# An eleventh expert buffer in a routed-expert decoder kernel, made from a smaller descriptor ring of the software queue

## The reference, cut to what matters

```python
h = h + mix                                  # retention, then dilated attention
hn = rmsnorm(h, ffn_norm[layer])
# per expert e, for the tokens routed to it:
hid = jax.nn.silu(xk @ w_gate[e]) * (xk @ w_up[e])     # 1024 -> 512
y   = hid @ w_down[e]                                  # 512 -> 1024
h = h + (sum of a token's two experts, weighted by the gates)
```

## Time and profile before

| | |
|---|---|
| median of 3 runs | 1400.17 us (1399.46 to 1400.95) |
| the profiled execution, first to last instruction | 1398.8 us |
| PE busy | 1075.8 us (77%) |
| DVE, ACT, POOL busy | 439.9, 343.5, 65.2 us |
| bytes moved, mean rate | 489.02 MB, 350 GB/s |
| mean granted TensorE clock | 0.899 of full |
| chain that ended last: DMA, PE | 46%, 45% of the span |

### The profile page before, as it was taken

How to read it: one execution, slowest core, us unless ns; L and a number is a source line. 1 busy time by engine, 2 the same in 40 slices (tenths; PEclk the granted TensorE clock), 3 DMA queues, 4 the chain that set the end, 5 groups by cost and what they waited for, 6 DMA issues and landing times.

```text
span 1398.8 us, 15978 instructions
## 1 busy us (share of the span) xinstructions
PE 1075.8 (77%) x6816; PEld 624.8 (45%) x6816; DVE 439.9 (31%) x863; ACT 343.5 (25%) x563; POOL 65.2 (5%) x120
## 2 busy tenths in 40 slices
PE   8999999666547666587999999999666646666586
PEld 8887885222212122132788877775222212122131
DVE  6845526010100101002876666736010100101001
ACT  4334524100001000011655555534100001000010
POOL 2000000000000000000300016300000000000000
PEclk9999999878888788899999999999988879788889
DMA  9655589999999999999755547699999999999997
GB/s 340 237 180 181 221 339 348 427 427 427 429 427 428 427 427 428 427 424 399 220 186 180 180 153 165 169 378 414 430 427 427 428 428 427 427 429 427 428 422 295
DMA packets 75785, 489.02 MB, mean 350 GB/s; under 512 B 6112, under 2 KB 6320, under 8 KB 51136
## 3 DMA queue, kind: packets, MB, share of 16 engines
q1 hardware_dynamic: 71296, 480.53, 84.6%
q0 software_dynamic: 4000, 7.36, 2.8%
q10 hardware_dynamic: 416, 0.07, 0.0%
HBM read 486.77 MB, written 1.17 MB: 349 GB/s over the span
## 4 chain that ended last, share of the span: by engine, by line
DMA 46%; PE 45%; DVE 3%; ACT 2%; issue 1%; SPq 1%; POOL 0%; DVEq 0%; ACTq 0%
DMA ring<-in_exp_up 11%; PE quad L1414 9%; DMA ring<-in_exp_gate 9%; PE quad L380 8%; PE quad L382 8%; PE quad L381 8%; DMA ring<-in_exp_down 6%; PE quad L1433 5%; DMA ring_more<-in_exp_down 5%; DMA ring_rows<-in_exp_up 4%; DMA ring_more<-in_exp_up 2%; DMA ring_rows<-in_exp_gate 2%; DMA ring_more<-in_exp_gate 2%; DMA ring_rows<-in_exp_down 2%; DMA ring<-in_ret_w_in 2%; PE bank L1323 1%
## 5 line engine op out<-in xcount | busy, mean ns | idle before, releaser
L1414 PE MATMUL quad<-ring,work 128*32 128x512 f32 x1136 | 246.3, 704 | 100.1 <-DMA ring_rows<-in_exp_up 24.9
L1414 PE MATMUL quad<-ring_more,work 128*32 128x512 f32 x512 | 186.8, 710 | 57.8 <-DMA ring<-in_exp_up 31.3
L1433 PE MATMUL quad<-ring,work 128*32 128x512 f32 x576 | 138.4, 723 | 57.4 <-DMA ring<-in_exp_down 21.8
L1566 DVE TENSOR_TENSOR work<-work,quad 128x512 f32<-128x512 f32 x16 | 11.0, 688 | 495.7 <-PE quad L1414 437.8
L1433 PE MATMUL quad<-ring_more,work 128*32 128x512 f32 x336 | 115.0, 706 | 58.9 <-DMA ring<-in_exp_down 58.0
L1414 PEld LDWEIGHTS quad<-ring,work 128*32 128x32 f32 x1136 | 61.0, 126 | 196.9 <-issue 186.9
L1575 DVE TENSOR_TENSOR h<-h,bank 128x512 f32<-128x512 f32 x64 | 44.0, 688 | 264.8 <-PE bank L1484 264.8
L1414 PEld LDWEIGHTS quad<-ring_more,work 128*32 128x32 f32 x512 | 42.7, 127 | 120.6 <-issue 113.0
L1503 ACT ACTIVATE work<-bank,gains 128x128 f32<-128x128 f32 x128 | 37.0, 368 | 227.1 <-PE bank L1323 227.1
L362 DVE TENSOR_TENSOR lo_b<-ring,hi_b 128x2048 fp32r<-128x2048 f32 (+1 forms) x40 | 86.2, 2181 | 15.9 <-ACT hi_b L356 15.9
L1433 PEld LDWEIGHTS quad<-ring,work 128*32 128x32 f32 x576 | 33.8, 130 | 108.5 <-issue 105.5
(11 more groups left out here) (341 smaller groups left out, 1825.1 us busy)
## 6 DMA issues: line engine op xcount, KB each, us to landing
ring<-in_exp_gate SPq DMA_DIRECT2D x39, 2048.0 KB, 29.2
ring<-in_exp_up SPq DMA_DIRECT2D x39, 2048.0 KB, 29.2
ring<-in_exp_down SPq DMA_DIRECT2D x34, 2048.0 KB, 28.4
ring_more<-in_exp_gate SPq DMA_DIRECT2D x20, 2048.0 KB, 27.7
ring_more<-in_exp_down SPq DMA_DIRECT2D x19, 2048.0 KB, 28.0
ring_more<-in_exp_up SPq DMA_DIRECT2D x18, 2048.0 KB, 29.2
ring<-in_w_kv SPq DMA_DIRECT2D x12, 2048.0 KB, 8.7
ring<-in_ret_w_in SPq DMA_DIRECT2D x11, 2048.0 KB, 8.8
```

Source lines behind the costliest of these rows:

```text
L1414: last = nc.tensor.matmul(bank[2 + kind][rows, :], m_x[:, k, rows], w[e][:, kk * FF:(kk + 1) * FF], start=(k == 0), stop=(k == KD - 1))
L1433: last = nc.tensor.matmul(bank[4 + nh][rows, :], m_hidT[:, k * P + e * SLOTS:k * P + (e + 1) * SLOTS], w[e][:, at:at + 512], start=(k == 0 ...
L1566: V.tensor_tensor(m_hid[0:M, :], m_sg[0:M, :], bank[3][0:M, :], ALU.mult).then_inc(s["hid_ready"], 1)
```

## The change

- `RING` goes from 10 to 11. The new slot, number 10 (`EXTRA_SLOT`, `ring_extra`), lies behind `work`; the arena grows by one tile of 16 KB per partition. Both `MOE_ORDER`s get slot 10 in front; in that of layer 0, slots 4 and 2 also change places.
- The room comes from the software queue's ring, which is built with 2048 bytes per partition (`SWDGE_RING`), and from five small tensors of the attention that move into free words of `work`.
- `AHEAD` becomes `(2, 1)`: in layer 0 the first two expert tiles (slots 10 and 6) are requested before `ret_w_out`. In layer 1, the first tile (slot 10) is requested before QKV 8; all ten others follow at the old place.
- One semaphore (`s_first`) is saved; the first quarter of the first tile now signals `s_fine[1]`, and the wait in `last_down_half` counts one more.

```diff
-RING = 10
+RING = 11
-MOE_ORDER = ((6, 9, 7, 0, 1, 5, 2, 4, 3, 8), (6, 5, 4, 1, 7, 8, 2, 0, 3, 9))
-AHEAD = 1
+MOE_ORDER = ((10, 6, 9, 7, 0, 1, 5, 4, 2, 3, 8), (10, 6, 5, 4, 1, 7, 8, 2, 0, 3, 9))
+AHEAD = (2, 1)
+AHEAD_OF_TILE = 8
+EXTRA_SLOT = 10
+SWDGE_RING = 2048
...
-        sb("arena", [P, FULL_RING * TILE + 4 * TT * D + WORK])
+        sb("arena", [P, FULL_RING * TILE + 4 * TT * D + WORK + TILE])
...
+        ring_extra = place("ring_extra", WORK_AT + WORK, [P, TILE])
...
             if ahead:
-                sp.wait_ge(r_o_done, 2 * RET_H)
-                for n in range(AHEAD):
+                if layer == 0:
+                    sp.wait_ge(r_o_done, 2 * RET_H)
+                else:
+                    sp.wait_ge(s_used, last_tile_in(EXTRA_SLOT, FIRST_MOE[1]) + 1)
+                for n in range(AHEAD[layer]):
                     load(n)
                 return
-            for n in range(AHEAD if layer == 0 else 0, RING):
+            for n in range(AHEAD[layer], RING):
...
-                pe.wait_ge(s_fine[nh], 16 * (layer + 2 - nh))
+                pe.wait_ge(s_fine[nh], 16 * (layer + 2))
...
-        d_ss = sb("head_squares", [P, 2, 8])
-        d_sd = sb("head_std", [P, 2, 8])
+        d_ss = area(3968, 2, 8)
+        d_sd = area(3984, 2, 8)
...
-        d_min = sb("row_min", [P, 2, TT, 2])
-        d_own_min = sb("own_class_min", [P, 2])
-        d_den = sb("row_sum", [P, 2, TT, 2])
-        d_inv = sb("row_sum_inverse", [P, LATE, TT, 2])
+        d_min = area(4000, 2, TT, 2)
+        d_den = area(4008, 2, TT, 2)
+        d_inv = area(4016, LATE, TT, 2)
+        d_own_min = work[:, 4032:4034]
...
                     sp.wait_ge(m[0]["over"]["used"], 3 * overflow + 1)
+                if i == AHEAD_OF_TILE:
+                    moe_sp(sp, 1, True)
                 load_tile(sp, FIRST_QKV + i, src, KD)
...
-    nc = _bacc.Bacc("TRN2", target_bir_lowering=False, num_devices=1)
+    nc = _bacc.Bacc("TRN2", target_bir_lowering=False, num_devices=1, dynamic_dma_scratch_size=SWDGE_RING)
```

More of the change, by code:

```diff
@@ L268, in slot @@
                 return ring_rows[:, :]
+            if at == EXTRA_SLOT:
+                return ring_extra[:, :]
             return ring[:, at, :] if at < FULL_RING else ring_more[:, at - FULL_RING, :]
@@ L273, in build @@
         s_gain0 = sem("mixer_gain_loaded")
-        s_first = sem("first_quarter_tile_loaded")
         s_rot = sem("rotation_tables_loaded")
@@ L280, in build @@
         s_used = sem("ring_tiles_used")
-        s_fine = [sem("second_quarter_of_first_tile_and_third_row_of_last_down_left"), sem("third_row_of_last_down_right")]
+        s_fine = [sem("second_quarter_of_first_tile_and_third_row_of_last_down_left"),
+                  sem("first_quarter_of_first_tile_and_third_row_of_last_down_right")]
         s_sq = sem("squares_summed")
@@ L345, in split_act @@
             if n == 0:
-                act.wait_ge((s_first, s_fine[0], s_ring[0], s_ring[0])[max(parts)], 16)
+                act.wait_ge((s_fine[1], s_fine[0], s_ring[0], s_ring[0])[max(parts)], 16)
             if 0 in parts:
@@ L2192, in _ @@
             first = ring[:, 0, :].rearrange("p (k c) -> p k c", k=KD)
-            for i, landed in enumerate((s_first, s_fine[0])):
+            for i, landed in enumerate((s_fine[1], s_fine[0])):
                 sp.dma_start(first[:, 2 * i:2 * i + 2, :], win[:, 2 * i:2 * i + 2, 0:COLS]).then_inc(landed, 16)
```

## The result

| | median, us | ratio to before, 95% interval |
|---|---|---|
| before, first runs | 1399.82 (4 runs) | |
| after, first runs | 1388.10 (4 runs) | 0.9918 (0.9906 to 0.9930) |
| after, second runs | 1389.20 (5 runs; before beside it 1399.57) | 0.9925 (0.9911 to 0.9939) |
| forecast | 1390.3 | 0.9930 |
| range of 8 in 10 | 1389.0 to 1396.8 | |

The change makes the kernel faster by 11.7 us in the first runs and 10.4 us in the second; the forecast was 9.87 us. Of the 2.2 us, 0.35 are in the starting point: the forecast started from 1400.17 us, the median of three runs, and with a fourth run the kernel before has 1399.82. So this study has two questions: whether the 9.87 us are where they were said to be, and where the others are from.

The account below looks back on a forecast made before the run. It took transfer to bound the expert layers. Terms -4.92 (layer 0), -4.95 (layer 1), 0 and 0 sum to -9.87 us: 1400.17 - 9.87 = 1390.3 us; range of 8 in 10: 1389.0 to 1396.8.

Parts of the forecast that it names:

- The bound: In both expert layers transfer is the bound: share 1.01, 4.92 and 4.95 us per tile, which a deeper ring can't quicken.
- Rival F: The loop bounds the expert layers, so eleven slots shorten every round: below 1389 us, down to 1326; chance 0.02.
- One tile per layer: In each expert layer one tile is carried before the saturated stretch: gains of 4.92 us and 4.95 us.
- Layer 0 with the ring's 0: Layer 0's gain of 4.92 us, taken together with the smaller descriptor ring's cost of 0.
- The boundary: From layer 0's experts to attention: QKV 0 lands 4.92 us earlier; QKV 2's new wait costs nothing, cover 10 us.
- Layer 1's early request: Expert tile requested before QKV 8: carried in idle time, QKV 8 later by 0 to 1 us, cost nothing.
- The smaller ring: GpSimd's smaller descriptor ring: cost bounded between nothing and 24.8 us, taken as nothing.
- At the start, little: Ring waits at the start hurt little: the last table is issued at 17.64 us, first needed at 59.57.
- Rivals C and D: C: one wait at attention's pair 2, up to 6.55 us, chance 0.10; D: waits in every batch, slower, 0.06.
- never blocks: In the attention at most some ten transfers are in flight, so the smaller ring never makes GpSimd wait.
- D's price: GpSimd waiting in all six attention batches adds 24.8 us, giving 1415.1 us.
- pair 2 has no cover: In the attention the chain runs through pair 2's bias loads, so a wait there goes straight onto the end.

Follow-up runs that it names:

- The first pair: The first traces of the kernel before and the changed kernel, whose first runs took 1399.82 and 1388.10 us.
- the second pair: The second traces of the kernel before and the changed kernel, both unedited: ratios to before 1.0002 and 0.9925.
- experiment 1: The kernel before and the changed kernel run again with no edit: ratios to before 1.0002 and 0.9925.

## Why the prediction was right, and where it was off

- **The bound.** Right. The expert layers run at 426 to 428 GB/s in every kernel with a share of 1.01, and the ring's length doesn't change the pace (4.92 and 4.91 us per tile). Rival F, that the ring's round trip is the bound, would have made each round shorter; it falls.
- **One tile per layer.** Right in place; right in size for layer 1, too small for layer 0. Layer 0 with the ring's 0: forecast 4.92 up to QKV 0's split, measured 5.50 and 5.32 in the two pairs and 5.35 over ten traces. The 4.60 and 4.57 of the stage alone leave out the start, and the start has no price of its own (see the smaller ring, below). With the router loads out of the stream it is 4.84. Layer 1: forecast 4.95, measured 6.80 and 4.95, and 4.91 over all fourteen traces with the lag of the slowest engine taken off. The first pair's 1.85 us too many are in this lag, which differs by 1.9 us between the two kernels there (6.08 and 4.18) and by 0.2 us in the second pair.
- **The boundary.** Right: QKV 0 moved with the stream and QKV 2's new wait is covered. The text priced the wait that the change made and not the one that the swap avoids, which is 5.9 us.
- **Layer 1's early request.** Costs nothing, as foretold, but no run shows that it is part of the gain: the eleventh slot gives the tile without it.
- **The smaller ring.** Here is the step that failed: "At the start, little", and with it a sum in which what GpSimd's small transfers take from the tiles stands at nothing. The ring does fill at the start, and what it holds back is the router loads, which stood among the first weight tiles. The first gate product comes 0.75 and 0.90 us earlier in the two pairs, 0.55 to 0.83 us with the ring alone. This isn't a further term of the sum, though: with the ring alone nothing of it is left at QKV 0's split. What the sum lacks is the 0.45 us or so by which layer 0 beats a tile as long as router loads stand in its stream. I looked only for who waits for the tables and not for what the small transfers take from the tiles beside them; layer 1's four, in the saturated stretch, cost 2.2 to 2.7 us in both kernels. The Trainium skill, DMA: Bandwidth & Descriptors, Issuing engines are not separate DMA queues, says that transfers issued by any engine run on the same sixteen DMA engines and interleave; the trace agrees (179 GB/s in 24 to 26 us against 302 with the small ring), and reading it that way would have put the sign at the start right.
- **Rivals C and D.** The changed kernel doesn't wait in the batches of pairs 2 to 7. It does wait once, 3.03 us, in the batch of pair 1, which follows pair 0's at once: "never blocks" was too much, and the prediction's own estimate that two batches don't fit was borne out. The attention isn't longer for it (296.83 against 296.99 us). D's price was too high as well, by the one trace there is: in the ring of 1280 bytes GpSimd stands ahead of five batches and the attention stays at 297.02 us. That pair 2 has no cover was right, but its batch starts with all old entries landed, so a ring that one batch fits doesn't touch it.
- **The range.** The sum of terms, corrected, is -5.35 - 4.91 = -10.3 us, or 1389.9 us by the forecast's reckoning, inside the range. So the 0.4 us that were mis-sized don't put the first median outside of it. Of its 2.2 us below the forecast, 0.35 are the starting point, 0.4 this term, and 1.4 stay unassigned. That is less than the interval of the ratio allows, +-1.7 us, so it can be chance. The range's lower end, 1.3 us under the forecast, was set with "some 1 us of drift" and had no room for it: two traces of the kernel before differ by 1.87 us, and its single runs go from 1398.28 to 1402.59. The forecast's ratio, 0.9930, is the upper end of the first interval and well inside the second.

What stays open: why the slowest engine lags by 3.7 us in one execution and 6.1 in another, and whether the change has a part in it; where the gain at the start goes in the kernels with ten slots; and how the router loads come to cost the kernel with ten slots 0.3 to 0.5 us more than the one with eleven (2.7 us against 2.2 and 2.4 at QKV 0's split).

## What to carry to other kernels

Where a stream of transfers is the bound, one more buffer is worth about one buffer's transfer time per saturated stretch (4.9 us of 4.9 in layer 1, 5.35 in layer 0), if idle transfer time lies ahead of it. Where in that time the load was issued made no difference at the two places tried. When a ring's length changes, work out anew which slot each stretch's last tiles lie in: the next stage's first load must not want the slot of the very last one (5.9 us here). Small transfers on another queue are paid by the large ones at their side; put them where the transfer engines are idle (some 2.3 us here for the four router loads of one layer).

## What the runs showed of the hardware

- A full descriptor ring of the software queue holds GpSimd at the next load, for 2.7 to 8.8 us at a time, and shows as idle time that ends by "issue". A ring of 2048 bytes per partition costs this kernel nothing that can be told (ratio 0.9996, 0.9987 to 1.0005); one of 1280 costs nothing in the stages of its one trace, while its median leaves it open.
- In the saturated stream the first and the last of a tile's sixteen completion marks both move on by 4.89 us per 2 MB tile, but they don't coincide: the last is 1 to 6 us behind the first. This distance stays the same to 0.1 us for up to 35 tiles and changes in steps, most of them upward: in the kernel before from 1.58 to 3.17 us between two tiles at 963.5 and 971.0 us, and in eleven of the fourteen traces by 0.46 to 1.55 us at one and the same tile of layer 1, n = 45 (1131 to 1144 us). A landing is the last mark. At the end of layer 1 such steps are paid in full (the table of experiment 1). At the end of layer 0 they aren't: in five traces with ten slots QKV 0 lands between 661.92 and 662.03 us, while the distance goes from 3.35 to 5.22 us; there it is the first marks that differ.
- The DMA share doesn't say how much is moved: in the kernel before it is 1.08 at 179 GB/s (24 to 26 us) and 1.05 at 387 (30 to 32 us), and only the rate shows that small transfers are among the large.
